# A six-layer transformer stack on one core: its on-chip buffers allocated in another order

## The chip, the core and the metric

The kernel runs on one core of a Trainium2 chip. The metric is the device time of one launch in microseconds (us). Each figure quoted for "before" is the median of three runs, and the trace that is read below comes from one further, profiled execution of the same program.

## What is computed

The input is one sequence of 256 tokens with 1,024 features in float32. It passes through six layers. Each is a feed-forward part, a mixer and a second feed-forward part, each added to the running sum `x`:

```
x = x + 0.5 * swiglu(rmsnorm(x), w_gate, w_up, w_down)      # 1024 -> 2816 -> 1024
x = x + mixer(rmsnorm(x))        # hgrn2, neighbourhood attention, MLA, hgrn2, then twice four gated branches
x = x + 0.5 * swiglu(rmsnorm(x), w_gate, w_up, w_down)
```

All weights together are about 586 MB and each is used once, in full float32 accuracy.

## The kernel before

**The weight stream.** All weights are packed into "slabs" of 128 partitions x 2,048 float32 (1 MB). SyncE's queue loads slab after slab into three slots of `raw`. ScalarE rounds a slab into `high` (line 1106), VectorE subtracts to get the rest, `low` (line 1546), each with three slots too. TensorE waits for `low`, multiplies, and frees the slots through `slab_done`.

**Three products for one.** To keep float32 accuracy with the one-pass type `float32r`, the activations are split in the same way (`xh` and `xl`, or the two halves of `ends`), and every tile of weights is multiplied three times by `three`, lines 425 to 427: high by high, high by low, low by high. In nearly all of them the stationary operand is a weight tile of 128 x 128 (512 bytes in each partition) and the moving operand is 256 tokens of `xh`, `xl` or `ends` (1,024 bytes in each partition). Only the projections to "values" turn this round: there a stretch of 512 columns (384 in the last two layers) of `high` or `low` moves, and a piece of `xh` or `xl` stands. In the table of groups the moving operand is named first: `prod<-xh,high` has `xh` moving.

**Other buffers.** `gs`, `sg` and `newt` hold a feed-forward block on its way through VectorE and ScalarE, `rstd` the norm's factors, `var` and `guess` the steps of an inverse root. `work` is the mixers' storage, ten regions of 8 KB in each partition; its matmuls (for instance line 683, the score products of the hgrn2 mixer) read both operands from `work`. `prm`, `cst` and `levels` are tables.

**Order of the work.** Each engine's program is written out by hand and in order, with semaphores between them. Nothing in it depends on where a buffer lies.

**Where a buffer lies.** `sb` takes the next free bytes of every partition, in the order of the calls. In front of the first call there are 1,024 bytes of scratch (the kernel asks for that size when it makes the program) and four constants of 32 bytes, so the first buffer, `raw`, begins at byte 1,152.

Of the kernel before, what the change touches and what calls it, by code (L numbers as in the profile page):

```python
# [10 lines left out]
U8 = mybir.dt.uint8  # L11
# [4 lines left out]
P = 128  # L16
T = 256
TT = T // P
D = 1024
KC = D // P  # L20
# [14 lines left out]
HALVES = (1, 2, 4, 8, 16, 32, 64)  # L35
# [49 lines left out]
def _params():  # L85
    at = 0
    for name, width in (
        [(f"norm{l}_{s}", KC) for l in range(LAYERS_1 + LAYERS_2) for s in range(3)]
        + [("hg_lb", LAYERS_1 * HG_HEADS), ("hg_g0", 1), ("hg_g3", 1), ("na_q", 1), ("na_k", 1)]
        + [("mla_qa", MLA_Q // P), ("mla_kva", MLA_KV // P), ("mla_qn", 1), ("mla_qr", 1), ("mla_kn", 1), ("mla_kr", 1)]  # L90
        + [(f"{n}{l}", w) for l in range(LAYERS_2) for n, w in (
            ("dw", 2 * CONV_K), ("dwb", 2), ("lng", 2), ("lnb", 2), ("sc", 2 * SC_K), ("swq", 1), ("swk", 1),
            ("fxq", 1), ("fxk", 1), ("bf", 1), ("sink", SWA_HEADS))]
        + [("relb", SWA_HEADS)]
    ):
        PARAMS[name] = (at, width)
        at += width
    return at


N_PARAMS = _params()
# [5 lines left out]
def _consts():  # L107
    at = 0
    for name, width in (
        [("ident", P), ("ones", P), ("heads", 38), ("whole", 38), ("ropes", 36), ("spread", 4 * P), ("rot", P)]  # L110
        + [("cos", T), ("sin", T), ("namask", GRID_W), ("fxmask", TT * T), ("select", FOX_HEADS)]
    ):
        CONSTS[name] = (at, width)
        at += width
    return at


N_CONSTS = _consts()
# [18 lines left out]
def build(nc, W, PRM, CST, START, RPB, XIN, OUT, TOE_ROWS, TOE):  # L137
    ctx = ExitStack()
    with ctx:
        def sb(name, shape, dt=F32):  # L140
            return ctx.enter_context(nc.sbuf_tensor(name, shape, dt))
# [5 lines left out]
        raw = sb("raw", [P, RAW, SLAB])  # L147
        high = sb("high", [P, HIGH, SLAB], F32R)
        low = sb("low", [P, LOW, SLAB], F32R)
        levels = sb("levels", [P, len(HALVES), P], U8)  # L150
        prm = sb("prm", [P, N_PARAMS])
        cst = sb("cst", [P, N_CONSTS])
        x = sb("x", [P, KC, T])


# [5 lines left out]
        oh, ol = ends[:, 0:KC, :], ends[:, KC:2 * KC, :]  # L161
        hidh = oh.rearrange("p (u a) t -> p u a t", u=4)[:, 0:2]
        hidl = oh.rearrange("p (u a) t -> p u a t", u=4)[:, 2:4]
        rstd = sb("rstd", [P, T])
        rstdT = sb("rstdT", [P, TT])
        var = sb("var", [P, 2, T])
        guess = sb("guess", [P, 2, T])
        newt = sb("newt", [P, 2 * T])
        sqsum = newt[:, 0:T]
        hid = newt.rearrange("p (a t) -> p a t", a=2)  # L170
        lbs = sb("lbs", [P, 2, HG_HEADS])
        oml = sb("oml", [P, 2, HG_HEADS])
        noml = sb("noml", [P, 2, HG_HEADS])
        lbt = sb("lbt", [P, 6 * HG_HEADS])
        zero16 = sb("zero16", [1, 4 * P], BF16)
        small = sb("small", [P, 8, 8])
        work = sb("work", [P, 10 * KC * T])

        acc = [ctx.enter_context(nc.psum_tensor(f"acc{i}", [P, 2, T], F32)) for i in range(4)]
        prod = [ctx.enter_context(nc.psum_tensor(f"prod{i}", [P, 2, T], F32)) for i in range(2)]  # L180
# [2423 lines left out]
```

## Time and profile before

| | us |
|---|---|
| median of 3 runs | 3561.61 (3558.04 to 3566.83) |
| the profiled execution, its own time | 3561.76 |
| its span, first to last instruction | 3560.0 |
| TensorE busy in it | 3451.9 (97%) |
| VectorE busy | 2436.1 (68%) |
| ScalarE busy | 1512.6 (42%) |
| mean granted clock of TensorE, share of full | 0.98 |

A matmul is pipelined: its duration, some 281 ns, overlaps that of the next. What it costs the engine is the distance from its start to the start of the next, called the interval below. It is read off the timeline, or as the length of a stretch in which the engine never stops divided by the matmuls in it.

### The profile page before, as it was taken

How to read it: one execution, taken by the hardware profiler on the slowest of the kernel's cores; microseconds unless marked ns; L12 is line 12 of the kernel's file. 1: busy time of each engine (PE TensorE's matmuls, PEld its weight loads, DVE VectorE, ACT ScalarE, POOL GpSimd, SP SyncE). 2: the span in 40 equal slices, each digit the busy share in tenths (PEclk: the TensorE clock that was granted, in tenths of full speed). 3: DMA queues.
4: the chain of work that ended last, by engine and by line, in shares of the span. 5: the costliest groups of instructions: out<-in, count | busy, mean ns of one | idle time of the engine just before them, and what ended most of it. 6: DMA issues, size and time to landing. Idle time of an engine off the chain costs nothing.

```text
span 3560.0 us, 66111 instructions
## 1 busy us (share of the span) xinstructions
PE 3451.9 (97%) x27753; PEld 3325.4 (93%) x27753; DVE 2436.1 (68%) x2671; ACT 1512.6 (42%) x1501; POOL 192.2 (5%) x148
## 2 busy tenths in 40 slices
PE   8999999999899998899999999999999999999999
PEld 8998899997699998699999889999989999999899
DVE  7668667664766667566767866766777666677766
ACT  4354334343534434443436433434444343344433
POOL 0000012000000000000000000000341000024100
PEclk9999999999999999999999999999999999999999
DMA  6543374544154553155454325454434545543454
GB/s 250 183 174 127 106 230 174 200 165 154 61 199 165 201 189 142 37 188 189 178 189 172 125 95 196 171 200 177 172 142 147 190 171 197 186 178 132 153 189 165
DMA packets 98920, 592.62 MB, mean 166 GB/s; under 512 B 25684, under 2 KB 26836, under 8 KB 27736
## 3 DMA queue, kind: packets, MB, share of 16 engines
q1 hardware_dynamic: 97280, 586.34, 45.9%
q10 hardware_dynamic: 1496, 4.20, 0.3%
q8 instruction: 110, 1.80, 0.2%
q14 instruction: 34, 0.28, 0.0%
HBM read 588.40 MB, written 2.11 MB: 166 GB/s over the span
## 4 chain that ended last, share of the span: by engine, by line
PE 88%; DVE 6%; ACT 3%; issue 2%; DMA 1%; SPq 0%; DVEq 0%; ACTq 0%
PE prod L425 20%; PE prod L426 20%; PE prod L427 20%; PE acc L426 7%; PE acc L425 7%; PE acc L427 7%; ACT high L1106 2%; DVE low L1546 2%; DVE work L1821 1%; PE acc L973 1%; PE acc L615 1%; PE acc L781 1%; PE stat L771 0%; DMA work<-start 0%; PE stat L626 0%
## 5 line engine op out<-in xcount | busy, mean ns | idle before, releaser
L425 PE MATMUL prod<-xh,high 128*128 128x256 f32 x5752 | 1621.7, 282 | 15.8 <-DVE low L1561 12.6
L426 PE MATMUL prod<-xl,high 128*128 128x256 f32 x5752 | 1618.3, 281 | 0.0
L1546 DVE TENSOR_TENSOR low<-raw,high 128x2048 fp32r<-128x2048 f32 x537 | 1241.3, 2312 | 550.9 <-ACT high L1106 548.9
L427 PE MATMUL prod<-xh,low 128*128 128x256 f32 x5752 | 1614.2, 281 | 0.0
L1106 ACT ACTIVATE high<-raw 128x2048 fp32r<-128x2048 f32 x550 | 1049.9, 1911 | 1012.3 <-PE prod L427 564.3
L425 PEld LDWEIGHTS prod<-xh,high 128*128 128x128 f32 x5752 | 1088.4, 189 | 34.4 <-issue 26.7
L427 PEld LDWEIGHTS prod<-xh,low 128*128 128x128 f32 x5752 | 1087.9, 189 | 0.0
L426 PEld LDWEIGHTS prod<-xl,high 128*128 128x128 f32 x5752 | 1087.3, 189 | 0.6
L426 PE MATMUL acc<-ends,high 128*128 128x256 f32 x2112 | 592.6, 281 | 0.0
L427 PE MATMUL acc<-ends,low 128*128 128x256 f32 x2112 | 590.8, 280 | 0.0
L425 PE MATMUL acc<-ends,high 128*128 128x256 f32 x2112 | 588.8, 279 | 0.7 <-DVE low L1546 0.7
L425 PEld LDWEIGHTS acc<-ends,high 128*128 128x128 f32 x2112 | 397.0, 188 | 1.2 <-issue 0.9
L427 PEld LDWEIGHTS acc<-ends,low 128*128 128x128 f32 x2112 | 397.0, 188 | 0.0
L426 PEld LDWEIGHTS acc<-ends,high 128*128 128x128 f32 x2112 | 396.6, 188 | 0.0
L1163 ACT ACTIVATE sg<-gs 128x512 f32<-128x512 f32 x120 | 75.8, 632 | 550.7 <-DVE gs L1695 550.7
L425 PE MATMUL prod<-ends,high 128*128 128x256 f32 x600 | 179.2, 299 | 22.0 <-DVE work L2203 15.6
L1695 DVE TENSOR_TENSOR gs<-prod,rstd 128x512 f32<-128x512 f32 x120 | 82.8, 690 | 147.5 <-PE prod L427 147.5
L426 PE MATMUL prod<-ends,high 128*128 128x256 f32 x600 | 175.6, 293 | 0.0
L427 PE MATMUL prod<-ends,low 128*128 128x256 f32 x600 | 175.4, 292 | 0.0
L1661 DVE TENSOR_TENSOR sg<-sg,gs 128x512 f32<-128x512 f32 x132 | 94.3, 715 | 92.9 <-ACT sg L1163 83.7
L425 PEld LDWEIGHTS prod<-ends,high 128*128 128x128 f32 x600 | 120.8, 201 | 28.9 <-DVE work L2203 17.2
L2354 POOL TENSOR_SCALAR work<-work,prm 128x256 f32<-128x256 f32 x2 | 1.1, 550 | 2484.4 <-DVE low L1546 2484.4
(224 smaller groups left out, 2802.9 us busy)
## 6 DMA issues: line engine op xcount, KB each, us to landing
raw<-stream SPq DMA_DIRECT2D x550, 1024.0 KB, 4.8
work<-rpb SPq DMA_DIRECT2D x16, 256.0 KB, 6.4
work<-bias_shifted ACTq DMA_DIRECT2D x2, 1024.0 KB, 4.7
cst<-consts SPq DMA_DIRECT2D x1, 1050.0 KB, 11.4
x<-x_in SPq DMA_DIRECT2D x1, 1024.0 KB, 4.9
raw<-stream SPq DMA_DIRECT2D x2, 512.0 KB, 7.1
work<-bias_by_distance ACTq DMA_DIRECT2D x2, 512.0 KB, 4.6
bias_shifted<-work ACTq DMA_DIRECT2D x1, 1024.0 KB, 5.7
```

What stands on the lines that cost most here:

```text
L425: nc.tensor.matmul(out, wh, ah, start=start, stop=False, **kw)
L426: nc.tensor.matmul(out, wh, al, start=False, stop=False, **kw)
L427: return nc.tensor.matmul(out, wl, ah, start=False, stop=stop, **kw)
L615: last = nc.tensor.matmul(acc[2 * (i % 2) + u][:, tt, :], lhs, rhs, start=(n == 0), stop=(n == terms - 1))
L781: last = nc.tensor.matmul(out, cst[rows, a + at * P:a + (at + 1) * P], guess[rows, q, 0:T], start=True, stop=True)
L973: last = nc.tensor.matmul(acc[2 * (i % 2) + u][:, tt, :], lhs, rhs, start=(n == 0), stop=(n == terms - 1))
L1106: nc.scalar.activation(high[:, s % HIGH, :], raw[:, s % RAW, :], ACT.Copy).then_inc(high_ready, 1)
L1163: nc.scalar.activation(sg[:, :, :], gs[:, :, :], ACT.Sigmoid).then_inc(sig_ready, 1)
L1546: v.tensor_tensor(low[:, s % LOW, :], raw[:, s % RAW, :], high[:, s % HIGH, :].bitcast(F32), ALU.subtract).then_inc(low_ready, 1)
L1661: v.tensor_tensor(sg[:, :, :], sg[:, :, :], gs[:, :, :], ALU.mult).then_inc(vec_step, 1)
L1695: v.tensor_tensor(gs[:, :, :], prod[0][:, :, :], over(rstd[:, :], 2), ALU.mult).then_inc(evac, 1)
L1821: last = v.tensor_tensor(blocks, blocks, factor, ALU.mult)
```

## The change

The same buffers with the same sizes are allocated in another order. Those whose size is a whole number of kilobytes come first (`raw`, `high`, `low`, `x`, `xh`, `xl`, `gs`, `sg`, `ends`, `work`, `var`, `guess`, `newt`, `rstd`), the others after them.

```diff
         raw = sb("raw", [P, RAW, SLAB])
         high = sb("high", [P, HIGH, SLAB], F32R)
         low = sb("low", [P, LOW, SLAB], F32R)
-        levels = sb("levels", [P, len(HALVES), P], U8)
-        prm = sb("prm", [P, N_PARAMS])
-        cst = sb("cst", [P, N_CONSTS])
         x = sb("x", [P, KC, T])
...
-        rstd = sb("rstd", [P, T])
-        rstdT = sb("rstdT", [P, TT])
+        work = sb("work", [P, 10 * KC * T])
         var = sb("var", [P, 2, T])
         guess = sb("guess", [P, 2, T])
         newt = sb("newt", [P, 2 * T])
         sqsum = newt[:, 0:T]
         hid = newt.rearrange("p (a t) -> p a t", a=2)
+        rstd = sb("rstd", [P, T])
+        rstdT = sb("rstdT", [P, TT])
+        levels = sb("levels", [P, len(HALVES), P], U8)
+        prm = sb("prm", [P, N_PARAMS])
+        cst = sb("cst", [P, N_CONSTS])
         lbs = sb("lbs", [P, 2, HG_HEADS])
...
         small = sb("small", [P, 8, 8])
-        work = sb("work", [P, 10 * KC * T])
```

The instructions of every engine, their order and their waits are the same in both programs, one for one; only addresses in them differ. The compiled programs give these addresses (bytes in each partition; "past" is the distance past the last multiple of 1,024):

| buffer | before | past | after | past |
|---|---|---|---|---|
| `raw` | 1,152 | 128 | 1,152 | 128 |
| `high` | 25,728 | 128 | 25,728 | 128 |
| `low` | 50,304 | 128 | 50,304 | 128 |
| `x` | 85,664 | 672 | 74,880 | 128 |
| `xh` | 93,856 | 672 | 83,072 | 128 |
| `xl` | 102,048 | 672 | 91,264 | 128 |
| `gs`, `sg` | 110,240, 112,288 | 672 | 99,456, 101,504 | 128 |
| `ends` | 114,336 | 672 | 103,552 | 128 |
| `rstd` | 130,720 | 672 | 208,000 | 128 |
| `var`, `guess`, `newt` | 131,776 and on | 704 | 201,856 and on | 128 |
| `work` | 139,584 | 320 | 119,936 | 128 |
| `cst` | 77,248 | 448 | 211,424 | 480 |

672 is 32 past a multiple of 64; 128, 320, 448 and 704 are multiples of 64; 128 is a multiple of 128 and not of 256.

## Rows read from the trace of the kernel before

**Rows 1.** The page: busy time of each engine, share, instructions.

```profile
PE 3451.9 (97%) x27753; PEld 3325.4 (93%) x27753; DVE 2436.1 (68%) x2671; ACT 1512.6 (42%) x1501; POOL 192.2 (5%) x148
```

**Rows 2.** The page: the chain that ended last, shares by engine.

```profile
PE 88%; DVE 6%; ACT 3%; issue 2%; DMA 1%; SPq 0%; DVEq 0%; ACTq 0%
```

**Rows 3.** Windows of TensorE: stretch, length, busy (matmuls), granted clock, DMA share, GB/s.

```profile
40.00:180.00 140.00, 139.93 (x1198) 1.00 0.53 195
400.00:575.00 175.00, 175.00 (x1477) 1.00 0.65 204
...
1715.00:1880.00 165.00, 165.00 (x1397) 1.00 0.53 191
2110.00:2280.00 170.00, 170.00 (x1451) 1.00 0.52 187
```

**Rows 4.** Groups by line and form: count, busy us, mean ns, idle before.

```profile
L425 PE MATMUL prod<-xh,high 128*128 128x256 f32 x5752 | 1621.7, 282 | 15.8 <-DVE low L1561 12.6 <-DVE xl L1599 3.2
...
L425 PE MATMUL acc<-ends,high 128*128 128x256 f32 x2112 | 588.8, 279 | 0.7 <-DVE low L1546 0.7
L425 PE MATMUL prod<-ends,high 128*128 128x256 f32 x600 | 179.2, 299 | 22.0 <-DVE work L2203 15.6 <-DVE work L1957 3.5 <-DVE ends L1769 1.9
```

**Rows 5.** Timeline of TensorE near 100 us: start, us, instruction.

```profile
99.81 0.28 PE L425 MATMUL prod<-xh,high 128*128 128x256 f32 x1
...
101.91 0.28 PE L425 MATMUL prod<-xh,high 128*128 128x256 f32 x1
```

**Rows 6.** Timeline of TensorE near 500 us.

```profile
499.77 0.28 PE L425 MATMUL prod<-xh,high 128*128 128x256 f32 x1
...
501.89 0.28 PE L425 MATMUL prod<-xh,high 128*128 128x256 f32 x1
```

**Rows 7.** Timeline near 306 us: 512 columns of `high` and `low` move.

```profile
306.30 0.40 PE L425 MATMUL prod<-high,xh 128*128 128x512 f32 x1
...
309.80 0.40 PE L425 MATMUL prod<-high,xh 128*128 128x512 f32 x1
```

**Rows 8.** Timeline near 1370 us: 256 columns of `high` and `low` move.

```profile
1369.56 0.28 PE L425 MATMUL prod<-high,ends 128*128 128x256 f32 x1
...
1370.61 0.28 PE L425 MATMUL prod<-high,ends 128*128 128x256 f32 x1
```

**Rows 9.** Timeline near 2530 us, where the granted clock is half.

```profile
2529.28 0.41 PE L427 MATMUL prod<-xh,low 128*128 128x256 f32 x1
...
2531.84 0.41 PE L427 MATMUL prod<-xh,low 128*128 128x256 f32 x1
```

**Rows 10.** Timeline near 355 us: score products, both operands in `work`.

```profile
355.27 2.05 PE L683 MATMUL acc<-work 128*128 128x128 f32 x16 [1.10 <-ACT work L1223]
357.08 0.37 PE L425 MATMUL prod<-xh,high 128*128 128x256 f32 x1
```

**Rows 11.** Groups of VectorE and ScalarE, 512 columns, all operands in SBUF.

```profile
L1661 DVE TENSOR_TENSOR sg<-sg,gs 128x512 f32<-128x512 f32 x132 | 94.3, 715 | 92.9 <-ACT sg L1163 83.7 <-ACT sg L1141 9.2
...
L2206 DVE TENSOR_TENSOR work<-work 128x512 f32<-128x512 f32 x8 | 5.5, 692 | 0.3
...
L2163 DVE TENSOR_TENSOR sg<-sg,rstd 128x512 f32<-128x512 f32 x2 | 1.4, 692 | 1.5 <-ACT sg L1141 1.5
...
L1141 ACT ACTIVATE sg<-gs 128x512 f32<-128x512 f32 x38 | 23.6, 621 | 26.9 <-DVE gs L1626 26.9
L1120 ACT ACTIVATE work<-work 128x512 f32<-128x512 f32 x32 | 19.9, 621 | 27.4 <-DVE work L1957 13.5 <-DVE work L1626 7.1 <-DVE small L2257 6.7
```

**Rows 12.** DMA issues: instructions, KB each, median us to landing.

```profile
raw<-stream SPq DMA_DIRECT2D x550, 1024.0 KB, 4.8
...
x<-x_in SPq DMA_DIRECT2D x1, 1024.0 KB, 4.9
```

## The prediction

> **What bounds the kernel now.** I read the page first: TensorE is busy 97% of the span, VectorE 68%, ScalarE 42% [rows 1], and the chain that ended last lies on TensorE for 88% of the span [rows 2]. A busy share says nothing about whether a matmul could be faster, because matmuls overlap. So the second view is the table of windows, over stretches of feed-forward work. There TensorE never stops, and the interval between starts follows by division: 140.00 us for 1,198 matmuls is 116.9 ns, 175.00 us for 1,477 is 118.5, 165.00 for 1,397 is 118.1, 170.00 for 1,451 is 117.2 [rows 3]. I looked at twelve such stretches: two gave about 117 ns and ten about 118 (the rows show two of each kind). The third view is the timeline, to see single starts. Near 100 us eighteen intervals take 2.10 us, 116.7 ns each [rows 5]; near 500 us eighteen take 2.12 us, 117.8 ns each [rows 6]. So there are two regular beats, 1.1 ns apart, on the same instructions and the same addresses. A beat holds from one stall of TensorE to the next.
>
> The group table gives the number of matmuls that this touches. Each of the lines 425, 426 and 427 has 5,752 + 2,112 + 600 of them with 256 moving columns [rows 4]; times three is 25,392. One nanosecond in the interval of all of them is 25 us, or 0.7% of the kernel. This is the only place where a change of addresses can move the total much: the DMA's share is 0.51 to 0.65 in these stretches [rows 3], so transfers are not late, and VectorE and ScalarE have slack.
>
> **What the change does.** It removes, adds and reorders no instruction and no wait. Every term is therefore a number of accesses times a change in their duration, and the question for each kind of access is whether it is faster at its new address. The table of addresses says what is new. First, nothing comes to lie on a multiple of 1 KB: because of the 1,152 bytes in front, everything comes to lie 128 bytes past one, which is also not a multiple of 256. Second, `raw`, `high` and `low` stay where they were. Third, `x`, `xh`, `xl`, `gs`, `sg`, `ends` and `rstd` go from 32 past a multiple of 64 to a multiple of 128, and `work` from 64 past a multiple of 128 to one.
>
> *Matmuls, moving operand.* The trace holds a direct comparison, since `high` already lies where `xh` will lie (128 past). In the value projections `high` and `low` move, 512 columns at a time: fifteen intervals take 3.50 us, 233.3 ns each, or 0.456 ns a column [rows 7]. With `xh`, 32 past a multiple of 64, it is 116.7 / 256 = 0.456 and 117.8 / 256 = 0.460 ns a column [rows 5, 6]. In the neighbourhood mixer the same swap exists with 256 columns: nine intervals take 1.05 us, 116.7 ns [rows 8], the very beat of `xh`. A moving operand at the new kind of address is thus streamed as fast as one at the old kind. Term: 25,392 x 0.0 = 0 us.
>
> *Matmuls, stationary operand.* Weight tiles keep their addresses in all 25,392. In the few with `xh` or `ends` standing [rows 7, 8] the standing operand is the one that is 32 past a multiple of 64, and the beat is the same. Term: 0.
>
> *What is above the ideal.* At half clock, 1.2 GHz, twelve intervals take 2.56 us, 213.3 ns [rows 9], exactly 256 columns at one a cycle, with `xh` at its old address. Half of that, 106.7 ns, would be one column a cycle at 2.4 GHz; the present beats are 10.0 and 11.1 ns above it. So there is a loss at full clock, but none at half clock. A start that cost an extra fetch would cost it at either clock. And the loss grows with the columns: 233.3 is 20.0 above 213.3 for 512. That makes it a limit on the rate of streaming and not a cost of where a row starts.
>
> *VectorE and ScalarE.* Additions of 128 x 512 take 692 ns with all operands in `work` (a multiple of 64) and 692 ns with `sg` and `rstd` (32 past one); ScalarE takes 621 ns from `gs` to `sg` and 621 ns within `work` [rows 11]. The 715 ns of line 1661 is the same form in the busy loop of the feed-forward part. If its 23 ns were a matter of address, all 132 would give 3 us, on an engine that is idle 92.9 us in front of that very line. Term: 0, with 3 us as the far bound on VectorE, hidden behind TensorE.
>
> *Transfers.* The 550 slab loads keep their target; each lands 4.8 us after issue, and one like it, into `x` at 672 past, takes 4.9 [rows 12]. `x`, `prm`, `cst` and the start tables are written once; the far bound is the 0.1 us between these two rows. Term: 0.
>
> The sum is 0 us against the profiled execution's own 3561.76 us (span 3560.0), which is 0.15 us from the median of the runs, 3561.61. I forecast 3561. The three runs before span 3558.04 to 3566.83, so 0.3%, about 11 us, is what a measurement of this kernel can tell from no change.
>
> **Rivals.** Four, priced on the same 25,392 matmuls.
>
> *The quick beat everywhere (faster, 0.09).* That the beat is either 116.7 or 117.8 ns with the same instructions looks like two reads of one memory that fall into one of two phases, and a phase could hang on the distance between the two operands' addresses, which does change (from 544 to 0 modulo 1,024 between `xh` and `high`). If the new distance always falls into the quick one, ten of twelve stretches gain 1.1 ns: 25,392 x 1.1 x 10 / 12 = 23 us, 3538 us. Against it: in one trace, with one set of addresses, both beats occur, so something other than addresses picks.
>
> *A third, slower beat (slower, 0.08).* The same mechanism with the other sign. Moving and stationary operand now begin at the same distance past a kilobyte, so both reads may meet in one part of the memory at the start of each matmul. One more step of 1.1 ns above the slower beat costs 1.1 ns in ten twelfths and 2.2 ns in two: 25,392 x 1.28 = 33 us, 3594 us. It decides from about 0.45 ns on. For it speaks only that nobody can see the memory's parts in a trace. Against it speak the score products: both operands lie in `work` at equal distances past a kilobyte already, and sixteen of them start within 357.08 - 355.27 = 1.81 us, 113.1 ns each [rows 10], no slower than the others. They move 128 columns in plain float32, so they bound it only roughly.
>
> *The whole loss is one of alignment (much faster, 0.04).* If the 10 to 11 ns above one column a cycle went away, 25,392 x 10.9 = 277 us would, giving 3285 us. Against it: `high` as the moving operand shows the same loss at the new kind of address [rows 7, 8]. The Trainium skill has a rule for this interval (TensorE: Matmul & The Clock Gate, section on the back-to-back issue gap): columns divided by 2.4, plus 2.5 ns, which is 109.2 ns for 256. The trace does not agree, at 116.7 and 117.8. Taken as what aligned operands would reach, it would return 25,392 x 8.2 = 208 us, an estimate from that page, giving 3353 us.
>
> *The change doesn't do what it says.* It leaves all at 128 past. If only true multiples of 256 or 1,024 are quick, nothing is gained here although something could be. That ends at 3561 too and is counted with the forecast.
>
> **How the numbers follow.** No change 0.74; quick beat 0.09, all gone 0.04, slow beat 0.08; 0.05 is left for luck in the beats and the clock, with no address behind it: the share of stretches at 116.7 ns can come out differently by some twelfths, 2.3 us each, so 11 us takes five of them; I give 0.02 to faster and 0.03 to slower. Faster 0.15, same 0.74, slower 0.11. The likeliest case's own range is 3551 to 3572. The overall range, 3537 to 3578, takes in the quick beat and half of the way to the slow one, and leaves out less than 0.2.
>
> **What the next profile would show.** Right: windows of feed-forward stretches at 117 to 118.5 ns, both beats present again, 233.3 ns for 512 columns, 692 and 621 ns in the named forms, `raw` landing after 4.8 us. Quick beat: all windows at 117. Slow beat: a beat of 119 ns or more in the timeline. Alignment loss: intervals near 107 or 109 ns. Wrong in a way I don't see: equal intervals and more idle time of TensorE between stages, which an address can't explain by any row here.

## The result: 1.5% slower, by 2.5 ns in each matmul

| | before | after |
|---|---|---|
| median of runs, us | 3560.31 (4 runs, 3558.04 to 3566.83) | 3617.03 (4 runs, 3615.75 to 3617.80) |
| span of the profiled execution, us | 3560.0 | 3613.9 |

The ratio is 1.0154, with a 95% interval of 1.0138 to 1.0169. The forecast of no change was wrong.

The page of the changed kernel (same columns as [rows 1] and [rows 2]) hides it: every share is within one point of what it was.

```profile
PE 3508.5 (97%) x27753; PEld 3383.8 (94%) x27753; DVE 2437.4 (67%) x2671; ACT 1511.8 (42%) x1501; POOL 191.3 (5%) x148
...
PE 88%; DVE 6%; ACT 3%; issue 2%; DMA 1%; SPq 0%; DVEq 0%; ACTq 0%
```

What is to be seen is in microseconds: TensorE is busy 56.6 us longer (3508.5 against 3451.9 in [rows 1]) and the span is 53.9 us longer. VectorE's total is up by 1.3 us and ScalarE's is down by 0.8. The time is inside the matmuls and not between them. The windows of TensorE, on the first three stretches of [rows 3] and one more (stretch, length, busy and matmuls, granted clock, DMA share, GB/s):

```profile
40.00:180.00 140.00, 139.73 (x1164) 1.00 0.54 188
400.00:575.00 175.00, 175.00 (x1444) 1.00 0.62 194
1715.00:1880.00 165.00, 165.00 (x1367) 1.00 0.50 180
2140.00:2290.00 150.00, 150.00 (x1242) 1.00 0.51 181
```

In the same 140 us only 1,164 matmuls start and not 1,198; in the 175 us it is 1,444 and not 1,477. The clock is granted in full in both. The timeline of the changed kernel near 100 and near 500 us (the starts of line 425, which is every third matmul) gives the interval:

```profile
99.76 0.28 PE L425 MATMUL prod<-xh,high 128*128 128x256 f32 x1
...
101.92 0.28 PE L425 MATMUL prod<-xh,high 128*128 128x256 f32 x1
...
500.03 0.28 PE L425 MATMUL acc<-ends,high 128*128 128x256 f32 x1
...
502.19 0.28 PE L425 MATMUL acc<-ends,high 128*128 128x256 f32 x1
```

Eighteen intervals take 2.16 us in both places: 120.0 ns, where [rows 5] have 116.7 and [rows 6] 117.8. The two beats of before have become one, slower than either. Take every three of matmuls at full clock, from the start of one line 425 to the next, in which nothing stalls. Their mean, for each matmul, is 119.96 ns for `xh` and 120.00 for `ends` against 117.40 and 117.55 before, and 98% and 100% of these threes take 360 ns (92% in the small group where `ends` moves into `prod`). That accounts for the time. The three groups of moving operand have some 23,600 of the 25,392 matmuls in such threes; the others are left out: 16,179 x 2.56 + 5,931 x 2.45 + 1,452 x 3.1 ns = 60 us. From it go 1.6 us that the projections to values gained (below) and 2.7 us by which TensorE is idle less. That leaves 56 us, against 53.9; the difference of 2 us is not explained.

The other engines' rows are the prediction's [rows 11] over again, at their new addresses:

```profile
L1661 DVE TENSOR_TENSOR sg<-sg,gs 128x512 f32<-128x512 f32 x132 | 94.0, 712 | 92.9 <-ACT sg L1163 83.7 <-ACT sg L1141 9.2
...
L2206 DVE TENSOR_TENSOR work<-work 128x512 f32<-128x512 f32 x8 | 5.5, 692 | 0.3
...
L1141 ACT ACTIVATE sg<-gs 128x512 f32<-128x512 f32 x38 | 23.6, 622 | 26.9 <-DVE gs L1626 26.9
L1120 ACT ACTIVATE work<-work 128x512 f32<-128x512 f32 x32 | 19.9, 621 | 28.4 <-DVE work L1957 14.1 <-DVE work L1626 7.6 <-DVE small L2257 6.7
```

### The profile page after: what moved, and what is told of

Read it like the earlier page. It is cut to its first block, busy times and chain, and to the rows that moved or that the text cites. A ratio compares the mean times of both kernels' runs of the same rounds, so it can differ in the third digit from the quotient of the medians.

```text
span 3613.9 us, 66111 instructions
## 1 busy us (share of the span) xinstructions
PE 3508.5 (97%) x27753; PEld 3383.8 (94%) x27753; DVE 2437.4 (67%) x2671; ACT 1511.8 (42%) x1501; POOL 191.3 (5%) x148
## 4 chain that ended last, share of the span: by engine, by line
PE 88%; DVE 6%; ACT 3%; issue 2%; DMA 1%; SPq 0%; DVEq 0%; ACTq 0%
PE prod L425 20%; PE prod L426 20%; PE prod L427 20%; PE acc L425 7%; PE acc L426 7%; PE acc L427 7%; ACT high L1106 2%; DVE low L1546 2%; DVE work L1821 1%; PE acc L615 1%; PE acc L973 1%; PE acc L781 1%; PE stat L771 0%; DMA work<-start 0%; PE stat L626 0%
## 5 line engine op out<-in xcount | busy, mean ns | idle before, releaser
L425 PE MATMUL prod<-xh,high 128*128 128x256 f32 x5752 | 1644.4, 286 | 14.6 <-DVE low L1561 12.5
L427 PE MATMUL prod<-xh,low 128*128 128x256 f32 x5752 | 1631.6, 284 | 0.0
L425 PEld LDWEIGHTS prod<-xh,high 128*128 128x128 f32 x5752 | 1108.8, 193 | 32.9 <-issue 27.2
L426 PEld LDWEIGHTS prod<-xl,high 128*128 128x128 f32 x5752 | 1108.9, 193 | 0.6
L427 PEld LDWEIGHTS prod<-xh,low 128*128 128x128 f32 x5752 | 1108.5, 193 | 0.0
L425 PE MATMUL acc<-ends,high 128*128 128x256 f32 x2112 | 597.8, 283 | 0.6 <-DVE low L1546 0.6
L426 PE MATMUL acc<-ends,high 128*128 128x256 f32 x2112 | 597.7, 283 | 0.0
L425 PEld LDWEIGHTS acc<-ends,high 128*128 128x128 f32 x2112 | 405.5, 192 | 0.8 <-issue 0.8
L426 PEld LDWEIGHTS acc<-ends,high 128*128 128x128 f32 x2112 | 405.5, 192 | 0.0
L427 PEld LDWEIGHTS acc<-ends,low 128*128 128x128 f32 x2112 | 405.5, 192 | 0.0
```

Source lines behind the costliest of these rows:

```text
L425: nc.tensor.matmul(out, wh, ah, start=start, stop=False, **kw)
L426: nc.tensor.matmul(out, wh, al, start=False, stop=False, **kw)
L427: return nc.tensor.matmul(out, wl, ah, start=False, stop=stop, **kw)
```

## Experiments

**The theories.** D: what counts is the distance between the start of the moving and that of the stationary operand, which the change took from 544 to 0 modulo 1,024. The rivals: A, the moving operand has to start 32 past a multiple of 64, as it did before; K, only true multiples of 1 KB are good, and 128 past one is not; O, the matmuls are slowed by the other buffers that moved. Each edit is one to three unused buffers between the real ones, which costs no instruction. Except for the last run, all start from the changed kernel. "Distance" is that of the moving buffer's start past that of the weights, modulo 1,024. A weight tile is 512 bytes wide, so the tiles of one buffer lie at two distances, 512 apart, and 32 and 544 name the same case. Each run's "before" is a run of the kernel before on the same chip; its medians there lay between 3561.9 and 3565.8 us, so times of different chips are compared only to within some 4 us.

**Where all buffers lie: two shifts of everything.**

```diff
+        sb("pad_raw", [P, 896], U8)        # second run: 32
         raw = sb("raw", [P, RAW, SLAB])
```

> 896 unused bytes in front of raw: every buffer of whole kilobytes now starts on a true multiple of 1,024, and all distances between buffers stay as in the changed kernel. Theory D (what counts is the distance between the moving and the stationary operand, now 0 modulo 512): the interval stays at 120.0 ns and the time at 3617 us. Theory K (only true multiples of 1 KB are quick, 128 past is the bad case): an interval at or below the 116.7 to 117.8 ns of before, 3560 us or less. Theory A (a moving operand must start 32 past a multiple of 64): 120.0 ns, 3617 us.

> 32 unused bytes in front of raw: every buffer moves by 32, so xh, xl and ends start 32 past a multiple of 64 again, as before, while their distance to high and low stays 0 modulo 512. Theory D: 120.0 ns, 3617 us. Theory A: back to 116.7 to 117.8 ns, 3560 us.

Measured: 3617.11 us with 896 bytes (ratio 1.0151, 1.0134 to 1.0168) and 3616.72 with 32 (1.0145, 1.0129 to 1.0162). Both traces repeat 120.0 ns. The windows of 60 to 170 us and 1160 to 1310 us of the first of the two:

```profile
60.00:170.00 110.00, 110.00 (x919) 1.00 0.52 188
...
1160.00:1310.00 150.00, 150.00 (x1242) 1.00 0.51 182
```

and of the second:

```profile
60.00:170.00 110.00, 110.00 (x919) 1.00 0.52 187
...
1160.00:1310.00 150.00, 150.00 (x1242) 1.00 0.52 182
```

The counts agree to the last matmul, and with those of the changed kernel (919 and 1,242 in the same stretches). K and A fall: where the buffers lie as a whole made no difference here, neither true kilobytes nor 32 past.

**One stream moved against the other.**

```diff
+        sb("pad_x", [P, 32], U8)
         x = sb("x", [P, KC, T])
...
+        sb("pad_gs", [P, 992], U8)
         gs = sb("gs", [P, 2, T])
```

> 32 unused bytes in front of x and 992 behind xl: x, xh and xl move by 32 and everything else stays as in the changed kernel, so the distance is 32 for xh and xl and 0 for ends. Theory D: the matmuls that move xh or xl (17,256) go back to 116.7 to 117.8 ns and those that move ends (8,136) stay at 120.0; the time falls by 17,256 x 2.2 to 3.3 ns, to 3560 to 3579 us. Theory O (the other buffers that moved, work, gs, newt, rstd, slow the matmuls by their own accesses): all stay at 120.0 ns, 3617 us.

Measured: 3579.08 us, ratio 1.0046 (1.0029 to 1.0063); mean interval 117.56 ns for `xh`, 119.86 for `ends`. The timeline of this kernel shows the step where the feed-forward part goes over from one operand to the other (line 427 here is the first of three):

```profile
107.24 0.28 PE L427 MATMUL prod<-xh,high 128*128 128x256 f32 x1
107.60 0.28 PE L427 MATMUL prod<-xh,high 128*128 128x256 f32 x1
107.95 0.28 PE L427 MATMUL prod<-xh,high 128*128 128x256 f32 x1
108.30 0.28 PE L427 MATMUL prod<-xh,high 128*128 128x256 f32 x1
...
110.08 0.28 PE L427 MATMUL acc<-ends,high 128*128 128x256 f32 x1
110.44 0.28 PE L427 MATMUL acc<-ends,high 128*128 128x256 f32 x1
110.80 0.28 PE L427 MATMUL acc<-ends,high 128*128 128x256 f32 x1
111.16 0.28 PE L427 MATMUL acc<-ends,high 128*128 128x256 f32 x1
```

Three matmuls take 0.353 us with `xh` (distance 32) and 0.360 with `ends` (distance 0), in one loop and with `work`, `gs` and the rest where the changed kernel has them, or exactly 1,024 bytes further on. O falls and D stands: moving `xh` and `xl` (and `x`) by 32 bytes gives back three quarters of the loss. The time is at the upper end of the 3560 to 3579 us expected.

A rival that no run was made for is that the other engines' reads and writes delay the matmuls. The trace of the changed kernel speaks against it: 433 of its threes with `xh` ran while VectorE and ScalarE both did next to nothing, with a mean of 360.0 ns, and 1,061 while both were busy nearly all the time, with a mean of 359.8.

**The sweep of distances.** The first run's edit; the others differ in the numbers (192, 64, 768; 384, 64, 576; 96, 64, 864; 320, 224, 480). `x`, `gs` and `sg` move along with `xh` and `xl`.

```diff
+        sb("pad_x", [P, 64], U8)
         x = sb("x", [P, KC, T])
...
+        sb("pad_ends", [P, 64], U8)
         ends = sb("ends", [P, 2 * KC, T], F32R)
...
+        sb("pad_work", [P, 896], U8)
         work = sb("work", [P, 10 * KC * T])
```

> x, xh and xl at distance 64 modulo 512 from the weights, ends at distance 128, all else as in the changed kernel. Theory D says that the two streams part by their distances; by how much is open: if only 0 is bad, both run at 116.7 to 117.8 ns and the time is 3560 us or below; if the memory's parts are 64 or 128 bytes wide and repeat, one or both stay at 120.0 ns. Theory A: both at 120.0 ns, 3617 us, since neither starts 32 past a multiple of 64.

> Distance of xh and xl to the weights 192, of ends 256, all else as in the changed kernel. Theory near (only a distance close to 0 modulo 512 is slow): both streams at 116.7 to 117.8 ns. Theory repeat (slow wherever the distance is a multiple of 128 or 64): ends near 119 to 120 ns, and xh there too if the step is 64.

> Distance of xh and xl to the weights 384, of ends 448, all else as in the changed kernel. Theory near: both streams at 116.7 to 117.8 ns. Theory repeat with a step of 128: xh near 119 to 120 ns, ends at 116.7 to 117.8.

> Distance of xh and xl to the weights 96, of ends 160, all else as in the changed kernel. Theory near: both streams at 116.7 to 117.8 ns, 3560 to 3566 us. Theory repeat: the same, since neither is a multiple of 64. A third beat near 113.3 ns, which the distance 64 showed in some of its matmuls, may come up here; neither theory forecasts it.

> Distance of xh and xl to the weights 320, of ends 544 (the distance of before), all else as in the changed kernel. If the pattern has period 512, ends runs like a distance of 32, at 116.7 to 117.8 ns, as before. Theory near: xh at 116.7 to 117.8 ns. Theory repeat with a step of 64: xh near 119 to 120 ns.

Measured, one run each, 3572.5, 3530.9, 3581.3, 3610.2 and 3515.1 us. The table has the mean interval of undisturbed matmuls at full clock, as above, and the share of threes that take 340 ns, a beat of 113.3 ns each. For `ends` it counts the feed-forward parts (`acc<-ends`). It includes the changed kernel (0), the one before (544; its `ends` is the 117.55) and the run with 32.

| distance | of `xh` and `xl`, ns | at 340 | of `ends`, ns | at 340 |
|---|---|---|---|---|
| 0 | 119.96 | 0% | 120.00 | 0% |
| 32 | 117.56 | 0% | | |
| 64 | 117.52 | 6% | | |
| 96 | 119.93 | 0% | | |
| 128 | | | 118.62 | 0% |
| 160 | | | 118.44 | 0% |
| 192 | 114.35 | 78% | | |
| 256 | | | 119.64 | 0% |
| 320 | 114.82 | 67% | | |
| 384 | 118.75 | 0% | | |
| 448 | | | 117.26 | 12% |
| 544 | 117.40 | 0% | 117.15, 117.55 | 0% |

"Only near 0 is bad" falls with 96 and 256, and "bad at every multiple of 64" falls with 64 and 192, and with 96 too, where it expected no loss. 0 and 256 are alike, and 128 and 384 are, which points to a pattern that repeats after 256 bytes. But 64 and 320 are not alike in their means (117.52 and 114.82), and 192 and 448 are not either (114.35 and 117.26). What agrees in these pairs is which beats occur, 340 and 353 ns for three; how often each occurs does not. At 448 even one buffer differs in itself: 12% at 340 ns in the feed-forward parts, 89% where `ends` moves into `prod`. And there is a beat of 113.3 ns that the kernel before never had.

**The good distances everywhere.** Four kernels. The edits:

```diff
# all at 192            # all at 320            # xh 192, xl 320, ends 192     # low 128 further on
+pad_x    192           +pad_x    320           +pad_x    192                  +pad_low  128
+pad_work 832           +pad_work 704           +pad_xl   128                  +pad_x     64
                                                +pad_ends 896                  +pad_work 832
                                                +pad_work 832
```

> Distance of xh, xl and ends to the weights all 192, all else as in the changed kernel. Theory D with what the sweep showed (distance 192: two beats, 113.3 and 117.8 ns, mean 114.4): 25,392 matmuls 3 ns quicker than in the kernel before, 76 us, so 3485 us and a ratio near 0.979. If ends does not follow xh at the same distance (because what counts is a pairing of another kind), 3530 us, as with ends at 256.

> All distances 320 instead of 192. Distance 320 gave xh a mean of 114.8 ns with ends at 544. Theory D with period 512: near 3495 us. If the pattern has period 256, 320 is 64, and the mean may lie anywhere from 114.8 to 117.5 ns, since the distance 64 showed 117.5: 3495 to 3560 us.

> xh at distance 192, xl at 320, ends at 192. If each pair of operands counts for itself, and both distances know the 113.3 ns beat, the middle matmul of three changes its phase and the choice between the beats may come out otherwise: between 113.3 ns throughout (3460 us) and 117.8 ns (3560 us).

> As all at distance 192 from high, but low lies 128 bytes further on, so its distance to xh and ends is 64. Theory D: the two matmuls of three around the load of low run by distance 64, mean 117.5 ns, and the time rises above that of the kernel with all at 192, by up to 25,392 x 2 ns = 50 us. If high alone counts, the time is that of all at 192.

Measured: all at 192, 3545.89 us, ratio 0.9943 (0.9926 to 0.9959), faster but far from the 3485 expected. All at 320, 3566.5, beyond the 3495 to 3560 expected. `xl` apart, 3555.0. And `low` moved, 3479.6, where I had expected it to lose. The timeline of the kernel with all at 192 shows why it fell short: near 100 us it has the quick beat, near 1,200 us the one of 117.8 ns. The first two lines are with `xh` and the last two with `ends`.

```profile
99.96 0.28 PE L427 MATMUL prod<-xh,high 128*128 128x256 f32 x1
...
102.68 0.28 PE L427 MATMUL prod<-xh,high 128*128 128x256 f32 x1
...
1200.23 0.28 PE L427 MATMUL acc<-ends,high 128*128 128x256 f32 x1
...
1202.35 0.28 PE L427 MATMUL acc<-ends,high 128*128 128x256 f32 x1
```

The first pair is 24 intervals in 2.72 us (113.3 ns), the second 18 in 2.12 (117.8). The windows show that it is the stretch and not the operand:

```profile
60.00:170.00 110.00, 110.00 (x973) 1.00 0.54 196
...
1160.00:1310.00 150.00, 150.00 (x1276) 1.00 0.53 189
```

Throughout the first stretch both operands keep the quick beat (113.0 ns by division), throughout the second neither does (117.6). Only 30% of its threes with `xh` are at 340 ns, where `xh` at the same distance had 78% with `ends` at 256. The timeline of that earlier run shows the difference (line 428 is the first of three):

```profile
1195.81 0.28 PE L428 MATMUL prod<-xh,high 128*128 128x256 f32 x1
...
1199.89 0.28 PE L428 MATMUL prod<-xh,high 128*128 128x256 f32 x1
...
1200.93 0.28 PE L428 MATMUL acc<-ends,high 128*128 128x256 f32 x1
...
1202.73 0.28 PE L428 MATMUL acc<-ends,high 128*128 128x256 f32 x1
```

There the beat changes from 113.3 ns (36 intervals in 4.08 us) to 120.0 (15 in 1.80) at the switch from `xh` to `ends`, with no stall between them, and with the next `xh` it is quick again. With all at 192, a beat survives the switch, and the slow one, once in, stays to the next stall. So how often a stream has the quick beat hangs on the other stream's distance too: `xh` at 320 had 67% with `ends` at 544 and has 5% with `ends` at 320. With `low` moved, so that the distance to `high` is 192 and to `low` 64, it is 98%.

**Is it the parting of `high` and `low`?** Four more runs. The first repeats the kernel with `low` moved; the others change only the numbers.

```diff
+        sb("pad_low", [P, 128], U8)        # then 128, 256, 896
         low = sb("low", [P, LOW, SLAB], F32R)
+        sb("pad_x", [P, 64], U8)           # then 896, 960, 192
         x = sb("x", [P, KC, T])
...
+        sb("pad_work", [P, 832], U8)       # then none, 832, 960
```

> The same kernel as the look with low 128 bytes further on: distance of xh, xl and ends 192 to high and 64 to low. If the even beat of 113.3 ns is a property of the addresses, every run lies at 3475 to 3485 us, ratio 0.976 to 0.979. If the look had luck in its phases, the runs scatter between 3480 and 3560 us.

> The changed kernel with low alone moved by 128 bytes: distance 0 to high, 896 to low. If a parting of high and low is enough, 113.3 ns and 3480 us. If each pair counts by its own distance, the pairs with high stay bad and those with low get better: an interval between 117.8 and 120.0 ns, 3565 to 3617 us.

> Distance 192 to high and 960 to low, low lying 256 bytes further on. If the pattern repeats after 256 bytes, this is the kernel with all at 192 again: both beats, 3540 to 3550 us. If it repeats only after 512 or more, it differs from it, and may be the quick beat throughout, 3480 us.

> Distance 64 to high and 192 to low, the mirror of the quick kernel. If the two roles are alike, 113.3 ns throughout and 3480 us. If the order of the three matmuls matters (high is loaded for two of them, low for one), it lies between 3480 and 3565 us.

Measured: 192 to `high` and 64 to `low` gives 3477.95 us again, ratio 0.9755 (0.9742 to 0.9767); one of its six runs took 9,092 us for a reason that nothing here shows, and is left out of the comparison. Its timeline near 100 us:

```profile
99.89 0.28 PE L428 MATMUL prod<-xh,high 128*128 128x256 f32 x1
...
103.97 0.28 PE L428 MATMUL prod<-xh,high 128*128 128x256 f32 x1
```

That is 36 intervals in 4.08 us, 113.3 ns, on another chip than the first time. With 0 to `high` and 896 to `low` it is 3600.1 us and 119.1 ns: a parting alone is not enough. With 192 and 960 (that is 192 modulo 256 again) it is 3542.1 us, and the shares of the quick beat (29% and 12%) are those of "all at 192" (30% and 13%): moving `low` by 256 bytes changes nothing in the feed-forward parts, as a pattern that repeats after 256 bytes would have it. The mirror, 64 to `high` and 192 to `low`, gives 3573.9 us, beyond the 3565 expected at most, and 117.9 ns with `xh`: the roles are not alike. In each three matmuls `high` is loaded twice and `low` once. And 42% of its threes with `xh` take 360 ns, where 64 or 192 to both weight buffers showed 1% at most. So the two distances act together, and the time is not a sum over the pairs, each by its own distance.

**The order of before, with the two distances.**

```diff
 # in the kernel before
+        sb("pad_low", [P, 128], U8)
         low = sb("low", [P, LOW, SLAB], F32R)
...
+        sb("pad_x", [P, 544], U8)
         x = sb("x", [P, KC, T])
```

> The kernel before with 128 unused bytes in front of low and 544 in front of x: xh, xl and ends at distance 192 to high and 64 to low, every other buffer in the old order and at other places than in the quick version. Theory D alone: 113.3 ns and 3475 to 3485 us, as there. If the other buffers' places count too, the time differs from 3478 us by more than 10 us.

Measured: 3476.36 us, ratio 0.9752 (0.9732 to 0.9773), within 2 us of the new order's 3477.95 though `work` and all tables lie elsewhere. Its windows, where the kernel before has 945 and 1,270 matmuls:

```profile
60.00:170.00 110.00, 110.00 (x973) 1.00 0.55 197
1160.00:1310.00 150.00, 149.95 (x1317) 1.00 0.51 182
```

So, to within these 2 us, the distances of TensorE's operands are all of it. Two unused buffers of 672 bytes together beat the kernel before by 2.5% and the changed one by 4%.

## Why the prediction was wrong

- **"A moving operand at the new kind of address is thus streamed as fast as one at the old kind. Term: 25,392 x 0.0 = 0 us."** This step failed. [Rows 7] and [rows 8] do have the moving operand where `xh` was to lie, but with `xh` or `ends` standing: the distance between the two was 544 there as well, with the other sign. I compared starts, one operand at a time, and took a pair to be as good as its parts. The pair that the change makes, both 128 past, stood nowhere among the main matmuls. The term is +2.5 ns, 60 us.
- **The bound from the score products.** [Rows 10] were used against a slower beat, as a pair at equal distances. They are plain float32 with 128 columns, and their mean interval in both traces is 113.2 ns, nearly twice as long for each column as that of the main matmuls. They bound nothing for `float32r` at one column a cycle. The prediction called the bound rough and then leaned on it.
- **The rival "a third, slower beat"** had the place, the cause and the sign: one beat, above both of before, from the equal distance, and the beat of 119 ns or more that it named as its sign is there. That two reads meet in one part of the memory, as it had it, no run shows. It was priced at one step of 1.1 ns, 3594 us, and measured at 120.0 ns and 3617. It had a chance of 0.08, because of the two points above. "Something other than addresses picks" the beat was half right: within one kernel two beats occur at the same addresses, and the addresses decide which beats there are. All at 192 has 113.3 and 117.8, all at 0 has only 120.0.
- **"That makes it a limit on the rate of streaming and not a cost of where a row starts."** Wrong in part. Of the 10.0 to 11.1 ns above one column a cycle, 3.4 to 4.5 come back at good distances; 6.7 ns, from 106.7 to 113.3, stayed in every run. The argument in front of it, "A start that cost an extra fetch would cost it at either clock", fails for the addresses: the changed kernel's distance costs 2.5 ns at full clock and nothing at half clock. Its timeline near 398 us, where the granted clock is half:

```profile
397.63 0.41 PE L425 MATMUL prod<-ends,high 128*128 128x256 f32 x1
...
399.55 0.41 PE L425 MATMUL prod<-ends,high 128*128 128x256 f32 x1
```

  Nine intervals take 1.92 us, 213.3 ns, as in [rows 9]; over 53 such threes the mean is 213.4 ns a matmul, and over 60 before it is 213.3. A loss that is absent at half clock can thus still be one of addresses.
- **Right:** nothing came to lie on a true kilobyte, and it would have made no difference (3617.11 us with 896 bytes in front); VectorE and ScalarE forms kept their 692 and 621 ns; slab loads still land after 4.8 us. The one load into `x`, 4.9 us before, took 5.3.
- **A slip in a sum:** the rule's 109.2 ns would return 10.9 - 2.5 = 8.4 ns and not 8.2, so 213 us and 3348 us. It changes no chance.

## What to carry to other kernels

Where TensorE is the bound and streams 4-byte operands at full rate, as here, the distance of the moving from the stationary operand is worth trying like a tile size: between the slowest of these kernels (0) and the quickest (192 to one weight buffer, 64 to the other) lie 6.7 ns in each matmul and 4% of the kernel, for a few hundred unused bytes. The quickest pair was found by trying, against my expectation, and nothing here forecasts it from the two distances. Round addresses were no virtue, and equal remainders were the worst choice. To judge such a change, read the interval between starts and compare pairs of operands; the busy share was 97% in all of them.

## What the runs showed of the hardware

- The intervals come in regular beats: three matmuls take mostly 340, 350, 353 or 360 ns; at 96, 128, 160 and 384 there are others too, from 352 to 363 ns. A beat lasts from one stall to the next where both moving operands have it, and ends at the switch of operand where they don't (`ends` at 256). With only the distances changed, the same instruction at the same granted clock goes from 113.3 to 120.0 ns.
- The Trainium skill (TensorE: Matmul & The Clock Gate, Part 2: What happens when you issue a matmul, step LDWEIGHTS) says that TensorE's two read ports are independent and that loading the next weights takes no bandwidth from the running matmul. The runs here don't bear that out: moving `low` alone, which is only ever stationary in these matmuls, by 128 bytes takes the kernel with all at 192 from 3546 to 3478 us. That the two reads meet in a part of the memory fits this and what repeats after 256 bytes, but is argued and not shown; no run here separates the two reads.
- Not every form wants the same distance. In the value projections, with 512 columns moving, the change helped. Timeline of the changed kernel near 302 us:

```profile
301.81 0.39 PE L425 MATMUL prod<-high,xh 128*128 128x512 f32 x1
...
303.85 0.39 PE L425 MATMUL prod<-high,xh 128*128 128x512 f32 x1
```

  Nine intervals take 2.04 us, 226.7 ns, where [rows 7] have 233.3. Over all undisturbed threes of this form the mean is 227.9 ns against 233.2 before, and it is 233.2 again in the run that moved `xh` by 32. With 384 columns it is 173.6 ns in both.
- Left open: why one pair of distances leaves a single beat and another two, what at a stall picks between them, and why 192 and 64 together have only the quick one.
